# Exchanging the halves of query and key heads by transfers instead of a permutation product in a decoder step

## What is computed

```
def rope(x, pos):
    half = HEAD_DIM // 2
    ...
    x1, x2 = x32[..., :half], x32[..., half:]
    return jnp.concatenate([x1 * cos - x2 * sin, x2 * cos + x1 * sin], axis=-1)

q = rope(rms_norm(zq.reshape(B, T, A_HEADS, HEAD_DIM), q_gain), pos)
k = rope(rms_norm(zk.reshape(B, T, A_KV_HEADS, HEAD_DIM), k_gain), pos)
```

## Time and profile before

| what | value |
|---|---|
| median of 3 runs | 2253.87 us (2252.63 to 2259.41) |
| the profiled execution's own time | 2259.57 us |
| its span, first to last instruction | 2257.8 us |
| granted TensorE clock, mean | 0.992 |
| TensorE matmul busy | 2237.8 us (99%) |
| VectorE / ScalarE busy | 1217.8 us (54%) / 952.4 us (42%) |
| weight loads (q1) / ScalarE's queue (q10) | 384.94 MB / 18.63 MB |

### The profile page before, as it was taken

The page is one execution under the profiler, slowest core; times in us unless marked ns, Lnnn a source line. Parts: engine busy times, 40 slices in busy tenths (PEclk is TensorE's granted clock), DMA queues, the critical chain, the costliest instruction groups (busy, mean ns, idle before and its releaser), DMA issues.

```text
span 2257.8 us, 43613 instructions
## 1 busy us (share of the span) xinstructions
PE 2237.8 (99%) x18226; PEld 2214.4 (98%) x18226; DVE 1217.8 (54%) x1294; ACT 952.4 (42%) x1059; POOL 18.1 (1%) x20
## 2 busy tenths in 40 slices
PE   7999999999999999999999999999999999999999
PEld 7999999999999999999999999999999999999999
DVE  5777556555555554444465366564555555544443
ACT  6545345334343434444353335454444334343332
POOL 0000000000000000000000020000000000000000
PEclk9999999999999999999999899999999999999999
DMA  6654465655555565555564384555565655555553
GB/s 210 234 174 138 129 189 173 193 180 184 182 182 183 171 194 178 181 180 171 188 197 142 124 249 152 187 179 184 169 196 175 190 180 184 181 183 187 189 189 128
DMA packets 217579, 405.13 MB, mean 179 GB/s; under 512 B 15440, under 2 KB 29392, under 8 KB 217312
## 3 DMA queue, kind: packets, MB, share of 16 engines
q1 hardware_dynamic: 201360, 384.94, 54.4%
q10 hardware_dynamic: 16112, 18.63, 2.5%
HBM read 395.67 MB, written 9.93 MB: 180 GB/s over the span
## 4 chain that ended last, share of the span: by engine, by line
PE 96%; DVE 1%; ACT 1%; DMA 1%; issue 0%; SPq 0%; ACTq 0%; DVEq 0%
PE ps L515 61%; PE ps L521 30%; DMA raw<-in_w_in_even 1%; PE ps L849 1%; PE ps L820 0%; PE ps L817 0%; ACT whi L405 0%; DVE wlo L414 0%; PE ps L859 0%; PE ps L596 0%; PE ps L887 0%; PE ps L614 0%; PE ps L605 0%; PE ps L550 0%; ACT xh L956 0%
## 5 line engine op out<-in xcount | busy, mean ns | idle before, releaser
L414 DVE TENSOR_TENSOR wlo<-raw,whi 128x1024 fp32r<-128x1024 f32 (+1 forms) x746 | 885.1, 1201 | 832.0 <-ACT whi L405 830.9
L405 ACT ACTIVATE whi<-raw 128x1024 fp32r<-128x1024 f32 (+1 forms) x746 | 765.2, 1038 | 906.1 <-PE ps L521 886.5
L515 PE MATMUL ps<-xh,whi 128*128 128x264 f32 x3904 | 802.2, 287 | 10.7 <-ACT whi L405 9.4
L515 PE MATMUL ps<-xl,whi 128*128 128x264 f32 x3904 | 794.1, 285 | 0.0
L515 PEld LDWEIGHTS ps<-xh,whi 128*128 128x128 f32 x3904 | 606.7, 190 | 19.1 <-DVE xl L1336 8.3
L515 PEld LDWEIGHTS ps<-xl,whi 128*128 128x128 f32 x3904 | 605.5, 190 | 0.0
L521 PE MATMUL ps<-xh,wlo 128*128 128x264 f32 x3904 | 559.0, 284 | 0.0
L521 PEld LDWEIGHTS ps<-xh,wlo 128*128 128x128 f32 x3904 | 507.3, 189 | 0.0
L515 PE MATMUL ps<-hh,whi 128*128 128x264 f32 x1920 | 391.3, 285 | 1.3 <-DVE gbuf L1326 1.3
L515 PE MATMUL ps<-hl,whi 128*128 128x264 f32 x1920 | 391.4, 285 | 0.0
L515 PEld LDWEIGHTS ps<-hh,whi 128*128 128x128 f32 x1920 | 298.3, 189 | 1.5 <-issue 1.5
(11 more groups left out here) (210 smaller groups left out, 589.3 us busy)
## 6 DMA issues: line engine op xcount, KB each, us to landing
raw<-in_w_gate SPq DMA_DIRECT2D x176, 512.0 KB, 4.1
raw<-in_w_up SPq DMA_DIRECT2D x176, 512.0 KB, 4.4
raw<-in_w_down SPq DMA_DIRECT2D x176, 512.0 KB, 3.7
raw<-in_w_in_even SPq DMA_DIRECT2D x72, 512.0 KB, 4.2
raw<-in_w_in_odd SPq DMA_DIRECT2D x66, 512.0 KB, 3.7
raw<-in_w_out_odd SPq DMA_DIRECT2D x32, 512.0 KB, 4.1
raw<-in_w_out_even SPq DMA_DIRECT2D x16, 512.0 KB, 4.6
raw<-in_w_out_even SPq DMA_DIRECT2D x32, 256.0 KB, 4.1
```

The source lines that it names most:

```text
L405: ins = act.activation(dst, src, ACT.Copy)
L414: ins = dve.tensor_tensor(dst, src, hi.bitcast(F32), ALU.subtract)
L515: pe.matmul(ps[:, bank + t, 0:T], whi[:, s, c:c + P], r[k0 + kk], start=first and kk == 0 and m == 0, stop=False)
```

## The change

The permutation product goes, with its constant (128 of 1368 columns) and its semaphore. In its place ScalarE issues four transfers at u = 8q + 12, once `qnorm` says that the tiles are scaled: each copies 32 partitions of all tiles of the group from `qk` to `gbuf`, to the partitions of the other half. VectorE waits at u = 8q + 13 for the four transfers, and multiplies `gbuf` in place by sines whose first half of each head now has the minus sign.

```
     c[:, C_BLK:C_BLK + P] = (r[:, None] // HD) == (r[None, :] // HD)
     half = HD // 2
-    for m in range(P):
-        if m % HD < half:
-            c[m + half, C_ROT + m] = -1.0
-        else:
-            c[m - half, C_ROT + m] = 1.0
...
-    c[:, C_SIN:C_SIN + T] = np.sin(ang)
+    c[:, C_SIN:C_SIN + T] = np.where(r[:, None] % HD < half, -1.0, 1.0) * np.sin(ang)
...
-            def qk_rot(q, c0, n):
-
-                pe.wait_ge(qnorm, q + 1)
-                for t in range(n):
-                    mm = pe.matmul(ps[:, 4 + t, 0:T], rot, qk[:, c0 + t, :], start=True, stop=True)
-                mm.then_inc(qrot, 1)
...
-                    if u == IN_UNITS * q + 13:
-                        qk_rot(q, c0, n)
...
+                    if u == IN_UNITS * q + 12:
+                        act.wait_ge(qnorm, q + 1)
+                        for h in range(4):
+                            to, fro = HD // 2 * h, HD // 2 * (h ^ 1)
+                            act.dma_start(gbuf[to:to + HD // 2, 0:nq, :], qk[fro:fro + HD // 2, c0:c0 + nq, :]).then_inc(d_rot, 16)
...
-                        dve.wait_ge(qrot, q + 1)
-                        dve.tensor_tensor(gbuf[:, 0:n, :], ps[:, 4:4 + n, 0:T], sin, ALU.mult)
+                        dve.wait_ge(d_rot, 64 * (q + 1))
+                        dve.tensor_tensor(gbuf[:, 0:n, :], gbuf[:, 0:n, :], sin, ALU.mult)
```

More of the change, by code:

```diff
@@ L83 @@
 NVEC = 104
-C_ID, C_BLK, C_ROT, C_COS, C_SIN, C_MASK, C_TRI, C_CNT = 0, 128, 256, 384, 648, 912, 1168, 1232
+C_ID, C_BLK, C_COS, C_SIN, C_MASK, C_TRI, C_CNT = 0, 128, 256, 520, 784, 1040, 1104
 C_ROW = C_CNT + 4 * 16
@@ L186, in decoder_step @@
         blk = cst[:, C_BLK:C_BLK + P]
-        rot = cst[:, C_ROT:C_ROT + P]
         ya, yb = used["hh"][0], used["hl"][0]
@@ L286, in decoder_step @@
         qnorm = sem("qnorm")
-        qrot = sem("qrot")
+        d_rot = sem("d_rot")
         qk_ready = sem("qk_ready")
```

## The result

| | before | changed |
|---|---|---|
| median, us | 2253.96 (2252.63 to 2259.41, 4 runs) | 2269.73 (2266.71 to 2272.38, 4 runs) |
| span of the profiled execution, us | 2257.8 | 2270.6 |
| mean granted clock | 0.992 | 0.989 |

The ratio is 1.0065, with a 95% interval of 1.0044 to 1.0086: slower by 0.65%, about 15 us (the medians differ by 15.8). The forecast was 2258.5 us, in a range up to 2262.5; the time lies above it, and in the direction that had a chance of 0.17.

The account below looks back on a forecast made before the run. TensorE, busy for 99% of the span, was taken as the bound. Exchanges of +0.5, +2.4 and -0.9 us plus 2.6 for the clock gave +4.6 us on 2253.87: 2258.5 us, range 2251.5 to 2262.5.

Parts of the forecast that it names:

- VectorE's tail: From the sines' start to TensorE's unit 8q + 16: VectorE's work up to moving the first tile, 5.46 us with TensorE's follow-on.
- the removal alone: Product gone with transfers hidden: -0.2 us at the first place, -0.9 at the third, -1.1 in all; rival's chance 0.14.
- First exchange: Ahead of unit 16: TensorE starts at 71.86 instead of 71.39, +0.5 us; bounds -0.2 and +1.9.
- X: Time at which VectorE's sine multiplication (L1461) starts; TensorE cannot start unit 8q + 16 before X + 5.46.
- upper bound, a landing of 3.5 us: First exchange: issues of 0.68 us, the last at 64.3, and this landing give X = 67.8, +1.9 us.
- Second exchange: Ahead of unit 24: X = 95.2, TensorE starts at 100.66 instead of 98.29, +2.4 us.
- Here the queue decides: Second exchange: the old value cache's copy stands ahead in the same queue, with nothing of it moving after 92.
- upper bound of 97.1: Second exchange: X if the exchange is as slow as a 6.8 us weight load, from 90.3; +4.3 us.
- case (c): Second exchange waits for the copy and the weight-load backlog; slower by over 0.3%, from X = 97.4; chance 0.17.
- Third exchange: At kv_T: landed by about 116, so TensorE does not wait, -0.9 us; holds while X is under 117.5.
- The clock: Behind unit 24's wait: 4.4 us of idle time drops TensorE's clock to half, +2.6 us; lower end 0.
- The sum: Three exchanges: +0.5 + 2.4 - 0.9 = +2.0 us; with the clock's +2.6, +4.6 us; forecast's chance 0.42.

Follow-up runs that it names:

- e4_no_transfers: Changed kernel without the twelve transfers and ScalarE's wait, so partners are wrong; ratio to the kernel before 0.9995 (0.9986 to 1.0004).
- e3_landing_not_awaited: Changed kernel with the same transfers sent from x to acc4 and VectorE not waiting for them; ratio to the kernel before 1.0017 (1.0007 to 1.0028).
- e9_loads_held: Changed kernel with SyncE holding weight loads of units 8q + 18 and later until the exchange has landed; ratio to the kernel before 1.0037 (1.0024 to 1.0050).
- e6_exchange_by_sync: Changed kernel with SyncE, not ScalarE, issuing the exchanges ahead of the load of unit 8q + 18; ratio to the kernel before 1.0025 (1.0015 to 1.0036).
- e1_copies_late: Changed kernel with the two old-cache copies issued at u = 40 and 42 instead of 18 and 20; ratio to the kernel before 1.0054 (1.0041 to 1.0067).
- e11_by_sync_copies_late: Changed kernel with SyncE issuing the exchanges and the cache copies at u = 40 and 42; ratio to the kernel before 1.0005 (0.9995 to 1.0016).
- e2_product_kept: Changed kernel with products of the old size put back on TensorE at u = 8q + 13, unread; ratio to the kernel before 1.0048 (1.0035 to 1.0061).

## Why the prediction was wrong

**Right.** Where the change is felt: units 16 and 24, through VectorE's tail. The tail from the start of the sines to TensorE was put at 5.46 us and is 5.48 (73.86 - 68.38) and 5.47 (108.86 - 103.39). That the removal alone is worth about 1 us: the rows of e4_no_transfers agree, its ratio can't resolve it. That the copies hold up the second exchange: by 2.0 to 2.9 us. That the clock falls: it did.

**First exchange: the step that failed first.** "So ScalarE's delay, not the landing, sets X = 66.4." The exchange was to take 4.15 us and took 6.4. The issue was priced at 0.40 us, from an issue that moves rows of all tiles, and is 0.61; with it alone the sines would start 4.9 us behind the scaling (e3_landing_not_awaited, e9_loads_held), 0.7 us later than forecast. The other 1.5 us are the landing, which the prediction had hidden behind the split. It was priced at 1.7 us, from a transfer at the very end of the kernel, when nothing else runs, on the ground that the engines were idle from 62 to 64. But the fourth was issued at 63.88, and the two weight loads at 63.19 and 64.39 share the engines with it: 4.5 us. Held back or queued behind, they leave 2.4 us (e9_loads_held, e6_exchange_by_sync). My own upper bound, a landing of 3.5 us as of the load issued in that stretch, was the right kind of row and nearer, though 4.5 us passed it too. The 2.3 us that the prediction worked out from the Trainium skill (DMA: Bandwidth & Descriptors, the two cost components) and set aside for the 1.7 us of its rows is what the undisturbed transfers took, 2.3 to 2.4 us; the page gives its fit for transfers issued by GpSimd, which none here is, so the agreement may be chance, and it has nothing for the 4.5 us. With TensorE's idle time of 4.5 us in place of 2.2 this is 2.3 us of error.

**Second exchange.** The forecast was 95.2 - 88.63 = 6.6 us, 9.6 were measured. Of the forecast, 5.3 us stand for the copy ahead, the exchange itself and its tail, and 1.25 for weight loads that take every second turn. With the copies alone in the way the exchange took 6.9 us (e9_loads_held), and the loads cost 2.7 more, so both terms were too small, by 1.6 and 1.4 us. And "Here the queue decides" is not so: without any copy the exchange still took 7.3 us (e1_copies_late). X passed the upper bound of 97.1 (88.63 + 9.56 = 98.2) and also the 97.4 from which case (c) was to decide. Case (c) named the right cause, the copy and the loads together; by e1, e9 and e11 each is worth 2.0 to 3.0 us, and within the scatter of single traces they add up.

**Third exchange.** "No wait: -0.9 us" was wrong, +1.1 us. It had X at 116, 3.8 us behind the scaling, by the same two prices; it took 7.2 us, one of the issues alone 1.43 us.

**The clock.** It was priced once, at 2.6 us, on the only long idle time in the trace, 5.3 us. It fell three times: at idle times of 4.5, 7.2 and 2.0 us, and not 3.8 us after TensorE stopped, as in the row that the prediction went by, but 3.7, 2.0 and 2.0 us after. The row of 1.08 us, taken as the bound where nothing happens, left open what lies between. In the runs, the clock stayed full with idle times up to 1.8 us, with 2.5 and 2.2 us in e11_by_sync_copies_late and with 3.0 in e9_loads_held, and fell with 2.5 in e6_exchange_by_sync and with 3.0 and 2.7 in e3_landing_not_awaited; it fell at every one of 3.8 us and more. So between 2.0 and 3.0 us either happened, and I can't say what decides.

**The sum.** Idle time of 4.54 + 7.19 + 1.99 - 0.26 = 13.5 us, less 4.45 of product, is 9.0; of the 20.5 us at half clock some 6 are idle, and half of the other 14 is lost, 7: together 16 us, against +15.7 at the first score. Forecast were 2.0 and 2.6. So the error of 11 to 12 us is 2.3 us at the first exchange, 2.8 at the second, 2.0 at the third and 4.4 in the clock behind them. The miss is not one of scatter: all three waits and the time at half clock came out longer in the trace than they were priced.

## What to carry to other kernels

Price the landing of a transfer by a row in which the same other queues are busy at the same moment, not by the quickest of its size, and look at what is issued during the whole exchange, not when it begins. An engine swap that takes work from the bound engine but puts a longer round trip into the same tight place can lose more than the work was worth, and here a pause of the bound engine cost up to nearly its own length again at half clock (1.7 us behind the 2.0 at the third place). The same transfers kept TensorE waiting nowhere at the three places when they were issued where the consumer waits for something else anyway, which here took only reordering factors that commute.

## What was not expected of the hardware

- Issuing a transfer over 32 partitions held the queue for 0.61 us, on ScalarE and on SyncE alike, where a weight load of 512 KB over 128 partitions holds it for 0.37 (0.47 to 0.58 right behind another issue). It can be much more: 1.43 us once in the changed kernel, 1.51 and 2.57 us in e6_exchange_by_sync.
- The clock can fall after TensorE has restarted: in e2_product_kept it did so 1.2 us behind the restart, and in e3_landing_not_awaited TensorE restarts at 101.69, and the clock is full over 102 to 103 and 0.51 over 103 to 104. The stretches at half clock between 60 and 160 us lasted 3.4 or 6.8 us each, but for the second of the changed kernel, 10.2.
- Giving TensorE unread work in its pauses (e2_product_kept) cost no time that the runs can show. That it shortens the stretches at half clock is possible and not shown.
- TensorE's same work behind the first score took 2123.5 to 2131.2 us, in step with its 14.3 to 30.7 us at half clock: that is most of the scatter that one has to read a gain of 1 to 3 us against.
